# The expert stage of a two-layer encoder: from a loop over experts to one pipeline over 56 chunks

## What is computed

```python
def moe_swiglu(h, router_w, w_gate, w_up, w_down):
    logits = (h @ router_w).astype(jnp.float32)
    top_vals, top_idx = lax.top_k(logits, TOP_K)                  # TOP_K = 2
    gates = jax.nn.softmax(top_vals, axis=-1)
    combine = jnp.sum(jax.nn.one_hot(top_idx, N_EXPERTS, dtype=jnp.float32) * gates[..., None], axis=-2)
    out = jnp.zeros_like(h)
    for e in range(N_EXPERTS):                                    # 8
        out = out + combine[..., e:e + 1].astype(h.dtype) * swiglu(h, w_gate[e], w_up[e], w_down[e])
    return out
```

## Time and profile before

| | us |
|---|---|
| median of 3 runs | 2155.3 (2154.8 to 2156.95) |
| profiled execution, span from first to last instruction | 2158.2 |
| of it the expert stage, from the first gather (1039.6) to the end | 1118.6 |
| TensorE busy | 1990.2 (92%) |
| VectorE busy | 1573.1 (73%) |
| ScalarE busy | 1200.2 (56%) |

### The profile page before, as it was taken

The page is one execution under the profiler, slowest core; times in us unless marked ns, Lnnn a source line. Parts: engine busy times, 40 slices in busy tenths (PEclk is TensorE's granted clock), DMA queues, the critical chain, the costliest instruction groups (busy, mean ns, idle before and its releaser), DMA issues.

```text
span 2158.2 us, 31392 instructions
## 1 busy us (share of the span) xinstructions
PE 1990.2 (92%) x11108; PEld 1687.2 (78%) x11108; DVE 1573.1 (73%) x2259; ACT 1200.2 (56%) x1602; POOL 73.5 (3%) x67
## 2 busy tenths in 40 slices
PE   7998989899999969898899999999999989999897
PEld 6986867799999948687777787777877778777785
DVE  7658575555558585755688897887978879788796
ACT  4543323343344533222577677776777777767674
POOL 1001011000000011020000000000000000000000
PEclk9987879899999989898799999999999999999998
DMA  9400000645454200014499898998989989889893
GB/s 291 144 25 1 1 1 21 201 160 173 151 184 138 74 1 1 1 59 147 145 338 325 298 365 285 339 329 296 362 285 339 330 295 364 302 318 329 300 362 131
DMA packets 239427, 442.95 MB, mean 205 GB/s; under 512 B 14320, under 2 KB 94240, under 8 KB 239216
## 3 DMA queue, kind: packets, MB, share of 16 engines
q1 hardware_dynamic: 238320, 437.87, 58.0%
q0 software_dynamic: 1024, 3.93, 0.5%
HBM read 439.61 MB, written 2.16 MB: 205 GB/s over the span
## 4 chain that ended last, share of the span: by engine, by line
PE 79%; DVE 14%; issue 3%; ACT 3%; DMA 0%; DVEq 0%; ACTq 0%; POOL 0%; SPq 0%; POOLq 0%
PE ps L1740 20%; PE ps L1742 20%; PE ps L1741 19%; PE ps L2123 2%; PE ps L2108 2%; DVE w_lo L1626 2%; PE ps L2127 2%; DVE cacc L1142 2%; PE ps L1753 2%; ACT w_hi L952 2%; DVE w_lo L1046 1%; PE ps L1902 1%; PE ps L2253 1%; PE ps L2235 1%; DVE acc L1667 1%
## 5 line engine op out<-in xcount | busy, mean ns | idle before, releaser
L1626 DVE TENSOR_TENSOR w_lo<-raw,w_hi 128x1024 fp32r<-128x1024 f32 x672 | 807.8, 1223 | 141.5 <-ACT w_hi L952 130.8
L952 ACT ACTIVATE w_hi<-raw 128x1024 fp32r<-128x1024 f32 x672 | 703.6, 1059 | 190.7 <-PE ps L1742 189.6
L1740 PE MATMUL ps<-w_hi,xe_hi 128*128 128x512 f32 x896 | 367.8, 410 | 37.9 <-DVE w_lo L1626 37.9
L1742 PE MATMUL ps<-w_lo,xe_hi 128*128 128x512 f32 x896 | 359.5, 401 | 0.0
L1741 PE MATMUL ps<-w_hi,xe_lo 128*128 128x512 f32 x896 | 359.3, 401 | 0.0
L1046 DVE TENSOR_TENSOR w_lo<-raw,w_hi 128x1024 fp32r<-128x1024 f32 (+1 forms) x164 | 183.5, 1156 | 123.6 <-ACT w_hi L698 123.6
L1740 PE MATMUL ps<-u_hi,w_hi 128*128 128x272 f32 x800 | 238.2, 298 | 15.5 <-DVE u_lo L1096 11.8
L1740 PEld LDWEIGHTS ps<-w_hi,xe_hi 128*128 128x128 f32 x896 | 171.6, 191 | 86.2 <-DVE w_lo L1626 48.2
L1742 PE MATMUL ps<-u_lo,w_hi 128*128 128x272 f32 x800 | 234.2, 293 | 0.0
L1741 PE MATMUL ps<-u_hi,w_lo 128*128 128x272 f32 x800 | 233.2, 291 | 0.0
L698 ACT ACTIVATE w_hi<-raw 128x1024 fp32r<-128x1024 f32 (+1 forms) x164 | 159.6, 1001 | 124.2 <-PE ps L1742 124.2
(11 more groups left out here) (383 smaller groups left out, 2874.5 us busy)
## 6 DMA issues: line engine op xcount, KB each, us to landing
raw<-in_moe_w_gate SPq DMA_DIRECT2D x112, 1024.0 KB, 5.1
raw<-in_moe_w_up SPq DMA_DIRECT2D x112, 1024.0 KB, 5.1
raw<-in_moe_w_down SPq DMA_DIRECT2D x112, 1024.0 KB, 4.9
raw<-in_w_in SPq DMA_DIRECT2D x30, 1024.0 KB, 5.8
raw<-in_w_out SPq DMA_DIRECT2D x16, 768.0 KB, 5.4
raw<-in_ffn_w_gate SPq DMA_DIRECT2D x11, 1024.0 KB, 5.1
raw<-in_ffn_w_up SPq DMA_DIRECT2D x11, 1024.0 KB, 5.2
raw<-in_ffn_w_down SPq DMA_DIRECT2D x8, 896.0 KB, 4.9
```

Source lines behind the costliest of these rows:

```text
L952: nc.scalar.activation(w_hi[(2 * NU + j) % SPLITS][:, :], raw[:, slot, PART * (j % 2):PART * (j % 2) + PART], ACT.Copy).then_inc(hi_ready, 1)
L1626: V.tensor_tensor(w_lo[(2 * NU + j) % SPLITS][:, :], raw[:, mslot(j // 2), PART * (j % 2):PART * (j % 2) + PART], w_hi[(2 * NU + j) % SPLI ...
L1740: mm(o, w[0], x[0], start=first, stop=False)
L1742: return mm(o, w[0], x[1], start=False, stop=last)
```

## The change

The expert stage is written as one straight sequence of 56 chunks on every engine, without loops.

- **Whole units.** ACT and DVE split 128 x 2048 at once into `m_hi` and `m_lo`, a ring of `RING` = 4 units in memory that the layers no longer use. The first three units are split at the end of layer 1's mixer: ACT's two before and one after the last `root`, DVE's three behind `model_norm`.
- **One order.** Every chunk n does gate and up of n, side steps, `tall` of n-1, `turn_hidden` of n, also from one expert to the next. Only the very last chunk has `tall` alone behind it.
- **Packed units.** The host lays the weights out as 336 blocks of 1 MiB in the order of use, 8 KB for each partition.
- **Pairs.** The tokens of two experts are gathered together (256 columns) into one of two buffers, in four steps of 8 matmuls, each in a chunk of its own between `up` and `tall`; so are the transposes of `sel` and the gates. The pair for experts 2 and 3 is gathered during experts 0 and 1, and so on; the empty ninth expert is gone.
- **Output of an expert.** ACT scales and rounds from PSUM in one instruction (`ye_high`), DVE forms the low part from PSUM in one (`ye_low`); `ye_f` is gone. The adds to `acc` are four separate steps between splits.
- **ScalarE's table** for silu is loaded once, ahead of the stage.

```diff
+RING = 4
-            def hi(q0, j, m):
-
-                slot = mslot(j // 2)
-                if j % 2 == 0:
-                    act.wait_ge(raw_full[slot], arrived[slot] + 16 * (m + 1))
-                act.wait_ge(half_used, q0 + j - SPLITS + 1)
-                nc.scalar.activation(w_hi[(2 * NU + j) % SPLITS][:, :], raw[:, slot, PART * (j % 2):PART * (j % 2) + PART],
-                                     ACT.Copy).then_inc(hi_ready, 1)
...
+            def hi(k):
+
+                slot = mslot(k)
+                act.wait_ge(raw_full[slot], arrived[slot] + 16 * (k // RAW_SLOTS + 1))
+                if 1 <= k <= 2:
+                    act.wait_ge(half_used, 2 * NU - 4 + 2 * k)
+                if k >= RING:
+                    act.wait_ge(m_used, k - RING + 1)
+                nc.scalar.activation(m_hi[k % RING][:, :], raw[:, slot, :], ACT.Copy).then_inc(m_hi_ready, 1)
...
+            nc.scalar.preload_act_table_set("silu_and_others")
...
+                for n in range(LAST + 1):
+                    e, c = divmod(n, CHUNKS)
+                    k0 = pas * MOE_UNITS + chunk_units(n)
+                    for j in range(4):
+                        if k0 + j > 2:
+                            hi(k0 + j)
+                        if j == 1 and n:
+                            if turn_step(n - 1) is not None:
+                                sel_t_copy(pas, turn_step(n - 1))
+                            if gather_step(n - 1):
+                                xe_copy(pas, *gather_step(n - 1), GATHER[0])
+                    if c == 1 and e:
+                        ye_high(pas, e - 1)
+                    if n:
+                        et_high(pas, n - 1)
+                        hi(k0 + 4)
+                        hi(k0 + 5)
+                    silu(pas, n)
+                et_high(pas, LAST)
+                hi(pas * MOE_UNITS + MOE_UNITS - 2)
+                hi(pas * MOE_UNITS + MOE_UNITS - 1)
+                ye_high(pas, NEXP - 1)
...
+                if l == DEPTH - 1:
+                    for k in range(3):
+                        lo(k)
...
+            def gather_step(n):
+
+                e, c = divmod(n, CHUNKS)
+                p = e // 2 + 1
+                at_ = {(0, 4): 0, (0, 5): 1, (1, 3): 2, (1, 4): 3}.get((e % 2, c))
+                return None if at_ is None or p >= PAIRS else (p, at_)
...
+                for u in range(MOE_UNITS):
+                    k = pas * MOE_UNITS + u
+                    if k < RAW_SLOTS:
+                        sp.wait_ge(lo_ready, 2 * (NU + k - RAW_SLOTS + 1))
+                    else:
+                        sp.wait_ge(m_lo_ready, k - RAW_SLOTS + 1)
+                    sp.dma_start(raw[:, mslot(k), :], a["moe_units"][u]).then_inc(raw_full[mslot(k)], 16)
```

The order of TensorE in the new stage, by function:

```diff
+                for n in range(LAST + 1):
...
+                    wide(k0, x, 0)
...
+                    wide(k0 + 2, x, 1)
+                    if c == 1 and e:
+                        pe.wait_ge(et_ready, pas * (LAST + 1) + n)
+                        scatter(pas, e - 1)
...
+                        turn_sel(pas, turn_step(n))
...
+                        gather(pas, p, step, GATHER[0])
+                    if n:
+                        tall(pas, n - 1)
+                    turn_hidden(pas, n)
+                tall(pas, LAST)
+                scatter(pas, NEXP - 1)
```

More of the change, by code:

```diff
@@ L2220, in tall @@
-            def tall(q0, j0, first, last_one):
-                for f in range(4):
-                    pe.wait_ge(lo_ready, q0 + j0 + f + 1)
-                    wh, wl = pair(j0 + f, 1)
-                    for b in range(2):
-                        cb = slice(512 * b, 512 * b + 512)
-                        last = three(ps[:, 3 + b, :], (et_hi[:, f, :], et_lo[:, f, :]), (wh[:, 0, cb], wl[:, 0, cb]),
-                                     first and f == 0, last_one and f == 3)
-                    last.then_inc(half_used, 1)
@@ L2231, in turn_hidden, with views, wide @@
-            def turn_hidden(item, c):
-                pe.wait_ge(eh_ready, 7 * item + c + 1 + 1)
-                pe.wait_ge(et_ready, 7 * item + c + 1)
+            def views(k, nk):
+                return tuple(w[k % RING][:, :].rearrange("p (k n) -> p k n", k=nk) for w in (m_hi, m_lo))
+            def wide(k0, x, bank):
+                for i in range(2):
+                    pe.wait_ge(m_lo_ready, k0 + i + 1)
+                    wh, wl = views(k0 + i, 4)
+                    for k in range(4):
+                        kt = 4 * i + k
+                        last = three(ps[:, bank, :], (x[0][:, kt, :], x[1][:, kt, :]), (wh[:, k, :], wl[:, k, :]),
+                                     kt == 0, kt == KT - 1)
+                    last.then_inc(m_used, 1)
@@ new lines, in tall @@
+            def tall(pas, n):
+                pe.wait_ge(et_ready, pas * (LAST + 1) + n + 1)
+                c = n % CHUNKS
+                for i in range(2):
+                    k = pas * MOE_UNITS + tall_units(n) + i
+                    pe.wait_ge(m_lo_ready, k + 1)
+                    wh, wl = views(k, 2)
+                    for j in range(2):
+                        f = 2 * i + j
+                        for b in range(2):
+                            cb = slice(512 * b, 512 * b + 512)
+                            last = three(ps[:, 3 + b, :], (et_hi[:, f, :], et_lo[:, f, :]), (wh[:, j, cb], wl[:, j, cb]),
+                                         c == 0 and f == 0, c == CHUNKS - 1 and f == 3)
+                    last.then_inc(m_used, 1)
@@ L2257, in gather_most @@
[L2257 to L2270 removed]
+                        c0 = P * (4 * (step % 2) + k)
+                        i = mm(o, src[:, t, c0:c0 + P], sel[:, t, :], start=(t == 0), stop=(t == 1))
```

476 lines of the change are left out of this document (209 added, 267 removed).

## The result

The changed kernel takes 2061.8 us (median of 4 runs, 2060.5 to 2063.0) where the kernel before takes 2155.9 (4 runs, 2154.8 to 2157.0): a ratio of 0.9562, 95% interval 0.9546 to 0.9577. The forecast was 2059. The profiled execution has a span of 2060.6 us, against 2158.2.

A forecast was written before the change was run, and what follows sets the result against it. TensorE bounds the kernel, with waits and slow clock around each expert's turn. Stage 1092.7 to 1000.6 us, earlier first weights and a 1.3 us shorter end give 2061.6, 96.6 less; from the median, 2059 us. Range 2046 to 2098.

The forecast's parts named there:

- 8 x 136.48 + 0.9: Stage before the change, first to last weights: eight experts at 136.48 us each plus 0.9, 1092.7 us in all.
- Of the 10.6 us per expert I leave nothing: Expert stage: all waits, slow clock and small restarts on TensorE, 10.6 of 136.48 us per expert, would go.
- Whole units: 128x2048 splits take 1.99 us on ACT, 2.30 on DVE; DVE's 15.2 us per chunk (upper bound 16.1) fits TensorE's 17.15.
- The ring: Four split units put each unit some 4 us early, so plain chunks have no wait and shorter side steps hide.
- The cause of the long gap: Chunk 2's splits queue behind ACT's copy of `sel_t`, which waits 5.10 us for TensorE; TensorE's gap is 2.73 us.
- Transfers: Packed 8 KB pieces move at least 408 GB/s against a mean need of 352, so loads drop out; packing costs zero.
- Loops: Straight-line code for some 4,300 stage matmuls on TensorE costs zero and gains nothing from missing branches.
- The start: First weights at 1047.3 us (bounds 1044.5 to 1048.5) instead of 1050.48, after a first gather at half clock.
- 1 and 5: Waits remain, or ACT and DVE still meet TensorE in step at each expert: 2095 us, chance 0.14 together.
- (2): The slow clock stays once per expert even without a gap: 1.5 us x 7, 2070 us, chance 0.08.
- (3): Transfers become the stage's bound: 2071 us at 348 GB/s, put at 2075, chance 0.06.
- Rival 4: Instruction fetches of the straight sequence stop TensorE, slower than before: 2170 us at 3 us each, chance 0.03.

The follow-up runs named there:

- unpacked kernel: The changed kernel with weight units loaded from the three original tensors in rows of 2 and 4 KB, not packed 8 KB rows: 2063.6 us, ratio 0.9586.
- the unrolled kernel: The kernel before with the expert stage's loops over experts and chunks written out straight on four engines: 2153.4 us against 2155.2, ratio 0.9994.
- the kernel without the long gap: The kernel before with ScalarE's copy of `sel_t` moved into chunk 6 and VectorE's copy of `gslot` to just before `select`: 2125.1 us, ratio 0.9877.

## Why the prediction came out as it did

**The sum.** From 2158.2 the forecast took 96.6 us. From the router's product on, where the two traces can be compared, 93.5 are gone. That the span came out 1.0 below the forecast's (2060.6 against 2061.6) is luck: the layers ended 4.1 us earlier in this execution. The terms of the sum, against what they measured:

| term | forecast | measured |
|---|---|---|
| first weights, earlier by | 3.2 | 4.45 |
| slow clock at their start | 2.9 | none |
| waits in the stage (0.9 + 5.5) | 6.4 | 6.4 |
| slow stretch behind the last wait | 1.5 | 1.9 |
| restarts | 1 | 5.8 |
| work taken out of the stage | 18.2 | 18.4 |
| stage | 1000.6 | 1003.8 |
| last weights to the end, less by | 1.3 | 0.1 |

Of the 3.2 us by which the stage is longer than forecast, 0.9 is the remainder of "8 x 136.48 + 0.9", which the sum did not carry on.

**Waits.** "Of the 10.6 us per expert I leave nothing" held for the waits and the slow clock. The step of the sum that failed is a size: the four transposes of a chunk, put at 0.35 us; what was missing there I had put among "the small change of restarts", which was to go. The 0.35 is read from the first transpose to the first weight matmul, and this stops too early. In the changed kernel the four start at 1412.58, 1412.69, 1412.80 and 1412.91, 0.109 apart, and then come:

```profile
1412.93 0.48 PE L1751 MATMUL ps<-m_hi,xe_hi 128*128 128x512 f32 x1
1413.25 0.39 PE L1752 MATMUL ps<-m_hi,xe_lo 128*128 128x512 f32 x1
```

The first weight matmul starts only 0.028 behind the fourth transpose, and the second 0.320 behind the first in place of 0.233. Together that is 0.348 us for one transpose and one weight matmul, against 0.109 + 0.233 = 0.342. So the 0.085, 56 times 4.8 us, are not a penalty of the change of form. They are nearly all the fourth transpose's own time, which shows one start later: the term is four times 0.109 = 0.44, not 0.35. By the first scatter matmuls of two experts that lie a pair apart (1191.17 and 1441.46) an expert takes 125.1 us, where 124.3 was forecast; 7 x 0.085 = 0.6 of the difference is this. The 4.8 us are the largest miss in the stage. They were hidden in part by another, the 2.9 us of slow clock at the start, which did not come: the slow stretch began 0.9 us into the gather and was over before its end (matmuls of 256 columns start 0.213 apart from 1036.2 to 1039.4, and 0.118 behind), so that the first weights ran at the full clock.

**Whole units.** Taken from the slope: 1.99 and 2.30 us. Measured: 1.92 and 2.29. VectorE's work per chunk of 15.2 us is right. That the upper bound of 16.1 would be borne as well was shown by running it with half units.

**The ring.** The table of times was right in its result, no wait in a plain chunk. As a reason it was too strong. It claimed that the ring of two was "too short to lay up work over a side step", and gave 4 us of lead to the ring of four. With three units nothing changes, and with two, in halves, 67.8 of the 93.5 us come all the same. So the order was the first cause, with some 45 us, and the ring the second, and 4 us of lead was more than the side steps needed.

**The cause of the long gap** was read rightly, but not in full: moving that copy and VectorE's of `gslot` gave 30 us, and the slow clock went with the gap. VectorE's copy was not named, and what either is worth alone was not run.

**Pairing.** The gather's pitch is 0.118 us for 256 columns, within the bounds and below the 0.122 taken.

**Transfers.** The mean need of 352 GB/s was right (354). Expected were over 408 GB/s while busy and a share under 0.9; it is 380 and 0.93. The 408 came from a stretch of 2 us, too short to carry over to a stage. The rest of the step, that packing costs and brings nothing, was tested and holds. The Trainium skill, "DMA: Bandwidth & Descriptors", Specifications, has about 358 GB/s as the limit of HBM for one core. The unpacked kernel comes near it, with 355 at a share of 98.5%; single windows of 20 us lie above it, with 367 in the changed kernel's second one above, and so does the packed rate while busy, 380. For this core the measurement decides.

**Loops.** Zero in the stage, by the unrolled kernel. But the edit had a place that I had not costed: the branch over the second pass, which now jumps a long way. VectorE's last instruction comes 1.84 us late, and it holds back the output: the last addition is done 8.3 us behind the last weights where it was 10.4. That, and not the scale, high and low steps, is where the 1.3 us of the end went: the scatter does start 3.0 us behind the last weights where it was 4.1.

**The start.** The first weights came 1.25 us earlier than forecast, since the slow clock covered only a part of the gather. The forecast's lower bound was 1044.5; counted from the router's product the measured start answers to 1046.0.

**The rivals.** None of the five happened: no wait for splits (1 and 5), no slow clock without a gap (2), no transfer in the way (3), no gap by "issue" in the stage (4). Rival 4's mechanism exists only at the one long branch.

## What to carry to other kernels

When one engine is to be kept busy, look first for the instruction in another engine's queue that waits longest for it, and move that: here two small copies were a third of the gain, and the order as a whole about half, before any buffer was added. Size a ring by the round trip of a buffer, and include what is queued behind the refilling instruction. Charge each gap of some microseconds on TensorE with its slow stretch. Read the price of a group of short matmuls up to the second start behind it, not the first.

## What the hardware showed

- A gap of TensorE cost more than its length: 4 us of idle time cost 6.2 (43.6 / 7), as 7 to 12 matmuls of 512 columns then started 0.427 us apart. The eight gaps of 2.7 us in the kernel before drew such a stretch too, 0.6 to 0.9 us behind their end, and seven of eight in the unrolled one. The waits of 1.57 us drew none there, and two of eight in the kernel without the long gap.
- Transposes of 128 columns start 0.109 us apart. The first matmul of 512 columns starts 0.028 behind the last of them and the second 0.32 behind the first in place of 0.233, each time, so four transposes cost 0.44 us and not the 0.35 up to the first start.
- Code in a straight line was fetched beside DMA engines busy at 93 to 98% without one stop: 34 fetches in 950 us. Behind the jump over the written-out second pass VectorE idled 1.61 to 2.52 us in every kernel that has it, and not in the kernel before.
- The same kernel reached its router's product at 1017.6, 1018.2 and 1022.6 us in three executions. A change of a few microseconds behind that point is seen in the parts of a trace sooner than in the medians.
